# Gated linear attention of one layer by chunks of 64 with summed logarithms, and two small computations moved

## The reference, cut to what matters

```
log_a = log_sigmoid(glr @ gla_w_gate2 + gla_b_gate2) / 16
b   = cumsum(log_a)                      # within a chunk of 64
q_e = q * exp(b);  k_e = k * exp(-b)
A   = where(causal, q_e @ k_e.T, 0)      # one masked 64x64 product
k_dec = k * exp(b_last - b);  S_next = exp(b_last) * S + k_dec.T @ v
o   = A @ v + q_e @ S
```

## Time and profile before

| | before |
|---|---|
| median of 3 runs | 3324.76 us |
| profiled execution, its own time | 3327.11 us |
| its span | 3325.3 us |
| TensorE busy | 3284.4 us (99%), 18046 instructions |
| VectorE busy | 2231.8 us (67%) |
| ScalarE busy | 1716.5 us (52%) |
| GpSimd busy | 401.4 us (12%) |
| DMA | 592.46 MB, 56.9% of 16 engines on its main queue |

### The profile page before, as it was taken

The page is one execution under the profiler, slowest core; times in us unless marked ns, Lnnn a source line. Parts: engine busy times, 40 slices in busy tenths (PEclk is TensorE's granted clock), DMA queues, the critical chain, the costliest instruction groups (busy, mean ns, idle before and its releaser), DMA issues.

```text
span 3325.3 us, 54997 instructions
## 1 busy us (share of the span) xinstructions
PE 3284.4 (99%) x18046; PEld 2828.9 (85%) x18046; DVE 2231.8 (67%) x3282; ACT 1716.5 (52%) x2550; POOL 401.4 (12%) x434
## 2 busy tenths in 40 slices
PE   8999999999999999999999999999999999999999
PEld 7888888887888878888888888888888888888888
DVE  6666666676655867666666677787566567666566
ACT  5444444454544655444444456774444445555554
POOL 1000000010123211000000001220243331100000
PEclk9999999999999999999999999999999999999999
DMA  6666666654555655666566555556545445555555
GB/s 225 188 198 189 189 188 185 190 183 146 172 161 161 197 168 162 191 188 188 188 190 189 187 176 176 192 177 183 161 154 160 152 156 173 184 166 182 176 171 165
DMA packets 280057, 592.46 MB, mean 178 GB/s; under 512 B 19856, under 2 KB 171664, under 8 KB 279840
## 3 DMA queue, kind: packets, MB, share of 16 engines
q1 hardware_dynamic: 278816, 587.12, 56.9%
q10 hardware_dynamic: 1152, 4.19, 0.3%
HBM read 589.14 MB, written 2.10 MB: 178 GB/s over the span
## 4 chain that ended last, share of the span: by engine, by line
PE 90%; issue 4%; DVE 3%; ACT 1%; POOL 1%; DMA 0%; SPq 0%; ACTq 0%; POOLq 0%; DVEq 0%
PE bank L545 41%; PE bank L544 10%; PE bank L547 10%; PE bank L584 8%; PE bank L586 8%; PE bank L585 8%; PE bank L772 2%; DVE w_low L1521 1%; PE bank L784 1%; DVE normed L1566 1%; ACT w_high L1042 1%; POOL work L2242 0%; PE bank L739 0%; PE bank L669 0%; DMA w_raw<-w_up1a 0%
## 5 line engine op out<-in xcount | busy, mean ns | idle before, releaser
L1521 DVE TENSOR_TENSOR w_low<-w_raw,w_high 128x1024 fp32r<-128x1024 f32 (+1 forms) x1120 | 1376.6, 1238 | 647.3 <-ACT w_high L1042 626.2
L1042 ACT ACTIVATE w_high<-w_raw 128x1024 fp32r<-128x1024 f32 (+1 forms) x1120 | 1166.3, 1044 | 785.7 <-PE bank L586 422.8
L545 PE MATMUL bank<-normed,w_high 128*128 128x512 f32 x3968 | 1266.5, 398 | 13.0 <-DVE w_low L1521 10.6
L545 PE MATMUL bank<-mixed,w_high 128*128 128x512 f32 x2432 | 772.2, 397 | 4.2 <-DVE increment L1553 4.2
L545 PEld LDWEIGHTS bank<-normed,w_high 128*128 128x128 f32 x3968 | 611.6, 189 | 14.5 <-issue 10.6
L544 PE MATMUL bank<-normed,w_low 128*128 128x256 f32 x1984 | 554.1, 279 | 0.0
L547 PE MATMUL bank<-normed,w_low 128*128 128x256 f32 x1984 | 551.8, 278 | 0.0
L584 PE MATMUL bank<-w_high,normed 128*128 128x512 f32 x1152 | 464.9, 404 | 1.1 <-DVE w_low L1521 1.1
L586 PE MATMUL bank<-w_high,normed 128*128 128x512 f32 x1152 | 451.5, 392 | 0.0
L585 PE MATMUL bank<-w_low,normed 128*128 128x512 f32 x1152 | 450.8, 391 | 0.0
L544 PEld LDWEIGHTS bank<-normed,w_low 128*128 128x128 f32 x1984 | 373.4, 188 | 90.2
(11 more groups left out here) (301 smaller groups left out, 2346.3 us busy)
## 6 DMA issues: line engine op xcount, KB each, us to landing
w_raw<-w_att SPq DMA_DIRECT2D x128, 512.0 KB, 3.7
w_raw<-w_up1a SPq DMA_DIRECT2D x64, 512.0 KB, 4.2
w_raw<-w_up1b SPq DMA_DIRECT2D x64, 512.0 KB, 4.1
w_raw<-w_up2a SPq DMA_DIRECT2D x64, 512.0 KB, 4.0
w_raw<-w_up2b SPq DMA_DIRECT2D x64, 512.0 KB, 4.0
w_raw<-w_rg SPq DMA_DIRECT2D x64, 512.0 KB, 4.2
w_raw<-w_hg SPq DMA_DIRECT2D x64, 512.0 KB, 3.6
w_raw<-w_hg SPq DMA_DIRECT2D x128, 256.0 KB, 2.8
```

Of the source, the lines that this page charges most:

```text
L545: last = nc.tensor.matmul(banks[b][:, :], hi, x, start=starts and k == 0, stop=stop)
L1042: A_(wh[slot][:, 0:width], raw[slot][:, 0:width], ACT.Copy).then_inc(wh_done, 1)
L1521: TT(wl[slot][:, 0:width], raw[slot][:, 0:width], wh[slot][:, 0:width].bitcast(F32), ALU.subtract).then_inc(wl_done, 1)
```

## The change

1. The rounds of the linear attention go from nine to three per head (0, 7 and 8 of the old numbers). VectorE sums the logarithms of the gates within chunks of 64 by one scan per head (step "prepare", with `chunk_start` as the factor that resets it), ScalarE takes exp(b) and exp(-b) (L1237 and L1238 of the new kernel), GpSimd multiplies q and k by them, and one product, masked by the sum of the level masks 0 to 6, gives all scores within a chunk. GpSimd then brings k to the chunk's end, and rounds 7 and 8 run as before. The rounds of the other phase with this code (hg, `heads == 2`) stay.
2. The gate logarithms of mixa are spread: exp at slot 13, log at unit 18, the sum at unit 25; the exp over the four heads goes (it is now per head in 1).
3. The rates' series is computed elsewhere: its first operation and its exp at the start of dn2a, the rest at the end of up2b.
4. GpSimd makes `chunk_start` at the start of the program and `chunk_mask` at the start of mixa.

```diff
-        AT_G = {0: [("values", 1), (4, 1)], 1: [(5, 1)], 2: [(6, 1)], 3: [(7, 1)], 4: [(8, 1)], 6: [("mix", 1)],
-                7: [("norm", 1), ("prepare", 0)], 8: [("gate", 1)], 9: [(0, 0), (1, 0)], 10: [("oturn", 1), (2, 0)],
-                11: [("store", 1), (3, 0)]}
+        AT_G = {0: [("values", 1)], 1: [(7, 1)], 3: [(8, 1)], 6: [("mix", 1)], 7: [("norm", 1), ("prepare", 0)], 8: [("gate", 1)],
+                10: [("oturn", 1)], 11: [("store", 1), (0, 0)]}
...
-        GATES = {1: [("gains", 0)], 5: [("table", 0)], 9: [("rank", 0)], 11: [("gate", 0)], 13: [("log", 0)]}
+        GATES = {1: [("gains", 0)], 5: [("table", 0)], 9: [("rank", 0)], 11: [("gate", 0)], 13: [("log_exp", 0)], 18: [("log", 0)],
+                 25: [("log_sum", 0)], 26: [("forget", 0)]}
...
-                    if step == 1:
+                    if step == (0 if heads == 1 else 1):
                         pe.wait_ge(dec["started"], it + 1)
-                    if step >= 2:
-                        pe.wait_ge(dec["placed"], it * 9 + (step - 1))
-                        pe.wait_ge(dec["updated"], it * 7 + (step - 1))
+                    if heads == 1 and step:
+                        pe.wait_ge(dec["updated"], updates(it, 1) + (step - 6))
+                        pe.wait_ge(dec["placed"], rounds(it, 1) + (step - 6))
+                    if heads == 2 and step >= 2:
+                        pe.wait_ge(dec["placed"], rounds(it, 2) + (step - 1))
+                        pe.wait_ge(dec["updated"], updates(it, 2) + (step - 1))
...
-                if step == "log":
+                if step == "log_exp":
                     act.wait_ge(gla["small"], 1)
                     own.did(A_(small_gate[:, :, :], small_gate[:, :, :], ACT.Exp))
+                if step == "log":
                     own.settle()
                     A_(small_gate[:, :, :], small_gate[:, :, :], ACT.Ln, bias=1.0).then_inc(gla["logged"], 1)
+                if step == "forget":
                     act.wait_ge(gla["forget"], 1)
-                    own.did(A_(FD[:, :, :], FD[:, :, :], ACT.Exp, scale=1.0 / 16))
-                    own.settle()
...
                     A_(B[:, 2, :], A[:, 1, :], ACT.Copy)
-                    A_(B[:, 0, :], A[:, 0, :], ACT.Copy)
-                    act.sem_inc(act_passed, 1)
-                    A_(Dm[:, 0, :], FD[:, i, :], ACT.Copy).then_inc(dec["prepared"], 1)
+                    A_(B[:, 0, :], A[:, 0, :], ACT.Copy).then_inc(dec["prepared"], 1)
+                    act.wait_ge(dec["summed"], it + 1)
+                    A_(Dm[:, 1, :], Dm[:, 0, :], ACT.Exp, scale=1.0 / 16)
+                    A_(Dm[:, 2, :], Dm[:, 0, :], ACT.Exp, scale=-1.0 / 16).then_inc(dec["grown"], 1)
...
+                if name == "dn2a":
+                    act.wait_ge(lru["rates"], 1)
+                    A_(poly[:, 1, :], poly[:, 0, :], ACT.Exp).then_inc(lru["rates"], 1)
...
+                    at = step if heads == 2 else (0, 7, 8).index(step)
+                    dve.wait_ge(dec["round"], rounds(it, heads) + (at + 1))
...
-                                ST[:, hd, 0:3:2, :], level_mask[:, step, :].unsqueeze(1).broadcast_to([P, 2, P]),
+                                ST[:, hd, 0:3:2, :], (level_mask[:, step, :] if heads == 2 else chunk_mask[:, :]).unsqueeze(1
+                                ).broadcast_to([P, 2, P]),
                                 b_in[:, hd * 2 * P:(hd + 1) * 2 * P].rearrange("p (b s) -> p b s", b=2))
                         last.then_inc(dec["placed"], 1)
+                if step == "prepare" and heads == 1:
+                    if not (isinstance(it, int) and it == 0):
+                        dve.wait_ge(dec["updated"], updates(it, 1))
+                    dve.sem_inc(dve_passed, 1)
+                    nc.vector.tensor_tensor_scan(Dm[:, 0, :], chunk_start[:, :], FD[:, bass.ds(it, 1), :].rearrange(
+                        "p a s -> p (a s)"), 0.0, ALU.mult, ALU.add).then_inc(dec["summed"], 1)
...
+                if name == "dn2a":
+                    a0 = COLS["rg_lambda_2"][0]
+                    lmb = vec[:, a0:a0 + KD]
+                    STT(out=poly[:, 0, :], in0=lmb, scalar=-1.0, in1=lmb, op0=ALU.mult,
+                        op1=ALU.min).then_inc(lru["rates"], 1)
+                if name == "up2b":
+                    lmb = vec[:, COLS["rg_lambda_2"][0]:COLS["rg_lambda_2"][0] + KD]
+                    dve.wait_ge(lru["rates"], 2)
+                    own.did(TS(poly[:, 2, :], poly[:, 1, :], 2.0, None, ALU.add))
+                    own.settle()
...
...
+                    TS(lru_c[:, 0, :], poly[:, 4, :], -8.0, None, ALU.mult)
+                    TS(lru_c[:, 1, :], poly[:, 4, :], 8.0, None, ALU.mult).then_inc(lru["rates"], 1)
...
-                    a0 = COLS["rg_lambda_2"][0]
-                    lmb = vec[:, a0:a0 + KD]
-                    STT(out=poly[:, 0, :], in0=lmb, scalar=-1.0, in1=lmb, op0=ALU.mult,
-                        op1=ALU.min).then_inc(lru["rates"], 1)
-                    dve.wait_ge(lru["rates"], 2)
-                    own.did(TS(poly[:, 2, :], poly[:, 1, :], 2.0, None, ALU.add))
-                    own.settle()
-                    own.did(nc.vector.reciprocal(poly[:, 3, :], poly[:, 2, :]))
...
+            own.did(nc.gpsimd.memset(chunk_start[:, :], 1.0))
+            own.settle()
+            nc.gpsimd.memset(chunk_start[:, 0:S:P // 2], 0.0).then_inc(filled, 1)
+            pool.wait_ge(filled, 5)
...
+                if heads == 1:
+                    last = Dm[:, 1, 63:S:64]
+                    pool.wait_ge(dec["grown"], it + 1)
+                    own.did(PT_(C[:, 0, :], B[:, 0, :], Dm[:, 1, :], ALU.mult))
+                    own.did(PT_(B[:, 2, :], B[:, 2, :], Dm[:, 2, :], ALU.mult))
+                    own.settle()
+                    pool.sem_inc(dec["started"], 1)
+                    pool.wait_ge(dec["round"], rounds(it, 1) + 1)
+                    PT_(B[:, 2, :].rearrange("p (c t) -> p c t", c=4), B[:, 2, :].rearrange("p (c t) -> p c t", c=4),
+                        last.unsqueeze(2).broadcast_to([P, 4, P // 2]), ALU.mult).then_inc(dec["updated"], 1)
+                    pool.wait_ge(dec["updated"], updates(it, 1) + 1)
+                    pool.wait_ge(dec["round"], rounds(it, 1) + 2)
+                    own.did(PT_(B[:, 2, 0:P // 2], B[:, 2, 0:P // 2], Dm[:, 1, P - 1:P].broadcast_to([P, P // 2]), ALU.mult))
+                    own.did(PT_(C[:, 0, 3 * P // 2:S], C[:, 0, 3 * P // 2:S],
+                                Dm[:, 1, 3 * P // 2 - 1:3 * P // 2].broadcast_to([P, P // 2]), ALU.mult))
+                    own.settle()
+                    pool.sem_inc(dec["updated"], 1)
+                    finish(it, heads)
+                    return
...
+                    pool.wait_ge(loaded, 16 * 3)
+                    own.did(PT_(chunk_mask[:, :], level_mask[:, 0, :], level_mask[:, 1, :], ALU.add))
+                    for level in range(2, LEVELS - 1):
+                        own.settle()
+                        own.did(PT_(chunk_mask[:, :], chunk_mask[:, :], level_mask[:, level, :], ALU.add))
+                    own.settle()
+                    pool.sem_inc(dec["masked"], 1)
```

More of the change, by code:

```diff
@@ L337, in block_kernel, with rounds, updates @@
         FEATURES = {"gla": 4, "hg": 8, "rg": 8}
+        def rounds(it, heads):
+            return it * 3 if heads == 1 else it * 9 - 6 * HEADS_G
+        def updates(it, heads):
+            return it * 2 if heads == 1 else it * 7 - 5 * HEADS_G
         def rec_end(it, heads):
@@ L732, in decay @@
                 if step == "mix":
-                    pe.wait_ge(dec["placed"], it * 9 + 9)
+                    pe.wait_ge(dec["placed"], rounds(it, heads) + (3 if heads == 1 else 9))
                     pe.wait_ge(rec["valued"], it + 1)
@@ L762, in decay @@
                             continue
-                        rhs = B if step == 0 else C
+                        rhs = B if step == 0 and heads == 2 else C
                         for b in range(NB):
@@ L837, in mixer @@
                     n, j = u // 24, u % 24
-                    if n == 0:
-                        for step, h in GATES.get(j, []):
-                            attention(step, h, False)
+                    for step, h in GATES.get(u, []):
+                        attention(step, h, False)
                     schedule(AT_A, 2, j, n, lambda s_, h: attention(*pair(s_, h), False))
@@ L1216, in prepare @@
                 if not (isinstance(it, int) and it == 0):
-                    act.wait_ge(dec["round"], it * 9)
+                    act.wait_ge(dec["round"], rounds(it, heads))
                 if heads == 2:
@@ L1787, in decay @@
                     b_in = (p_a, p_b)[step % 2]
-                    dve.wait_ge(dec["round"], it * 9 + (step + 1))
+                    at = step if heads == 2 else (0, 7, 8).index(step)
+                    dve.wait_ge(dec["round"], rounds(it, heads) + (at + 1))
                     if step:
```

(5 more changed lines are left out.)

61 lines of the change are left out of this document (30 added, 31 removed).

## The result

| | before | changed |
|---|---|---|
| median | 3325.11 us (4 runs, 3324.29 to 3326.62) | 3300.91 us (4 runs, 3300.82 to 3301.96) |
| ratio, 95% interval | | 0.9926 [0.9914, 0.9938] |
| profiled execution, its span | 3327.11, 3325.3 us | 3301.96, 3300.2 us |
| TensorE busy, instructions | 3284.4 us, 18046 | 3267.8 us, 17950 |
| GpSimd busy | 401.4 us | 367.3 us |

Forecast 3301.5, measured 3300.9. A second set of five runs of the same kernel gave 3302.98 (3301.28 to 3303.77), beside a before of 3325.11; all nine runs together have a median of 3301.96. So the gain is 22 to 24 us, 23.2 was forecast.

What follows compares the result with a forecast made beforehand. TensorE, busy 99% of the span, was taken as the bound. Terms 4.75 + 2.7 + 3.85 + 2.5 + 10.56 + 0.67 − 0.8 − 1.0 = 23.2 us took 3324.76 to 3301.5, range 3294 to 3310.

Steps and rivals of the forecast that it cites:

- Mixa: Before the score step, spreading logarithms cuts TensorE's 5.90 us stop to 1.15: +4.75 us, and +2.7 from full clock.
- The loss at the turn: First head group's weighted sum in mixa: TensorE, now arriving at full clock, stops there; charged −0.8 us, bounds 0 and −1.01.
- Rg: Before the spread in phase rg, removing the series ends the whole stop: +3.85 us, and +2.5 of half clock.
- Rounds: Linear attention: 24 rounds fewer, 0.45 us each, or 0.37 beside a turn; +10.56 us, bounds 8.9 and 26.6.
- Slot 7: Added scan, load and exps beside the previous head's end, heads 1 to 3: hidden, margin 0.4 us, cost 0, bound 6.3.
- Dn2b: Moved series delays VectorE's weights, so TensorE stops before dn2b's fourth unit: −1.0 us, bounds 0 and −5.1, clock kept.
- The clock: Behind mixa's and rg's stops: half clock disappears, giving 2.7 and 2.5 us; a stop near 1.01 us keeps full clock.
- 1: Remaining stops in mixa and dn2b both still lose the clock, 2.5 to 2.7 us each: −5.2, 3306.7 us; chance 0.15.
- 2: Linear-attention rounds are worth their records' mean duration, 26.6 us in place of 10.56: 3285.5 us; chance 0.08.
- 3: Slot 7's chain is longer than worked out, 1.0 us past TensorE for three heads: −3.0, 3304.5 us; chance 0.09.
- 4: Series not covered at all at dn2b: −5.1 in place of −1.0, and −2.5 of clock: 3308.1 us; chance 0.06.
- 5: Slower than before: the VectorE, ScalarE, GpSimd path stops TensorE at round 0, slot 11, heads 1 to 3; 3333.0 us; chance 0.02.

Runs made afterwards that it cites:

- the spare products: Changed kernel with two spare fp32 128x128 products on TensorE at each of the 24 places where a linear-attention round was removed; 3312.07 us, ratio 0.9963.
- the kernel with the rounds alone: Changed kernel with the gate logarithms together again at slot 13 and the rates' series back in phase rg; 3308.77 us, ratio 0.9950.

## Why the prediction was right

**Mixa.** Right in kind in each term: the stop of 1.15 us (1.02), the clock kept behind it, the clock's 2.7 us back. The loss at the turn was mis-sized, 0.44 where 0.8 was charged.

**Rg.** Right: no stop, 6.38 us for 6.35. Undoing this part alone brought the stop back at 3.18 us, its cause was VectorE's series.

**Rounds.** Right in kind and 5% low in size: 0.44 us a round as a mean in the sum, 0.46 measured by the spare products. The price of 0.37 at slot 10 was the term that was mis-sized: there the spare round cost 0.45 to 0.47 as well. The wait of 0.67 us was worth 0.94. Pricing by the pitch of the weight stream was the choice that mattered: records' durations would have given 26.6.

**Slot 7.** Right in result and, for its margin, by luck to a degree: the chain was 0.2 to 0.3 us longer than worked out, since a duration taken from a quiet stretch (1.20) didn't hold beside a busy GpSimd (1.62). 0.13 us were left of the 0.4.

**Dn2b.** Right: a stop of 0.86 us, 1.12 to 1.14 us with the slower products behind it, charged 1.0. Not foreseen was the 0.34 us lost at 1254.21.

**The clock.** Here the reasoning was weaker than its outcome. I took "1.01 kept, 1.81 lost" as a property of the length. Across all fourteen traces, the one of before included:

| stop | traces with it | sum of (1 − granted clock) behind it, us |
|---|---|---|
| up to 1.65 us (0.8 and more) | 14, several each | none |
| 1.81 to 1.83 us | 14 | 1.7 in 10, none in 4 |
| 1.87 to 2.64 us, at 25 us in the opening | 6 | 1.7 in 1, none in 5 |
| 2.31 us | 14 | 1.7 in 9, none in 5 |
| 3.17 to 3.39 us | 5 stops in 4 traces | none twice, 1.7 twice, 3.4 once |
| 3.65 to 5.90 us | 5 stops in 2 traces | 1.7 twice, 3.4 three times |

(Where part of the half clock lay in the stop itself, as at 809.01, the work lost was less than the sum, 2.7 of 3.4.) The stops that the change left lie in the row without loss, so the forecast held. But the 2.7 and 2.5 us that I counted back are what one execution of before had lost, and before was traced only once; another may have lost less there, as stops of 3.65 and 4.48 us did in a variant. This fits with medians that gain 22 to 24 us while the two profiled executions differ by 25.1, and no second trace of before shows it. Of the 25.1, 0.8 us stood in the opening before any part of the change acted: TensorE's first matmul began at 10.64 before, at 9.92 and 10.67 in two traces of the changed kernel, and at 9.48 in one variant. That the first median came within 0.6 us of the forecast is in part luck: terms that were 0.3 to 0.9 us off in both directions made up for each other, and the second set of the same kernel came 1.5 above it.

**Rivals.** 1 (the small stops lose the clock) refuted by every trace. 2 refuted by the spare products. 3 refuted for this kernel, with 0.13 us to spare. 4 refuted, 0.86. 5: GpSimd had over 6 us of room as worked out (973.42 to 980.06), and round 0 never waited for it, but for the variant that pushed its work behind the gate.

## What to carry to other kernels

Price work on the engine that bounds the time by how much later the next instruction of its stream starts, not by busy time or record durations. Before charging a stop with a clock penalty, look at more than one execution: here stops up to 1.65 us never cost it, stops from 1.8 to 3.4 us did or did not (the one of 2.31 us both, in two executions of the same kernel), and those of 3.65 us and more always did, so a change that brings a stop under the first bound is worth more than its idle time on average, and a difference of one or two steps of 1.7 us between two traces proves nothing of the edit. When durations from a quiet stretch are added up to a margin below 0.5 us, ask which engine will run beside them.

## What the runs showed of the hardware

VectorE and GpSimd slow each other on float32 operations in SBUF: `w_low` took 1.62 us in place of 1.23 with the second of GpSimd's two multiplications beside its first 0.55 us, and the two multiplications took 1.58 and 1.72 us in place of 0.75 when they ran beside two `w_low`. In the first case GpSimd's operation had started 0.20 us ahead of the `w_low` and took its usual 0.75; in the second the `w_low` had started first, and both took longer (the pair 2.90 us in place of 2.34). What the two share was not tried.

The sum of 1 − granted clock behind a stop was 0, 1.7 or 3.4 us and hardly anything between, whatever the length of the stop. What decides between none, one and two is left open: two executions of one kernel with the same 3.39 us stop, ended at 805.66 and 806.13, had sums of 1.7 and 3.4. The place in time counted from the first instruction doesn't decide it either: the same stop in the kernel with the rounds alone ended at 806.11, 0.02 us from the second, and kept the clock. No run here moved a stop alone.
